# The head of an encoder step: no dummy products on TensorE ahead of the first turns, and a wait in front of GpSimd's first low halves

## The chip, the cores and the metric

The kernel runs on one core of a Trainium2 chip. The metric is the time of one execution in microseconds (us) on the device. Runs without the profiler give a median; one more execution was taken with the profiler, and all rows below come from that one. Engines: TensorE (PE, with PEld its weight loads), VectorE (DVE), ScalarE (ACT), GpSimd (POOL), SyncE (SP). TensorE's clock is granted at one of two levels, 2.4 GHz (1.00 in the rows) and 1.2 GHz (0.50).

## The reference

One inference step of an encoder layer over 256 prompt frames and 64 sample frames (320 tokens of width 1024), everything in float32:

```
x  = layer_norm(x, ln_in_g, ln_in_b)                  # the head: what this study is about
z  = x @ w_in                                         # q, k, v, u, vs, ga, gb
A  = chunk_attention(q, k, v, relative bias, cache)   # 8 heads x 64
B  = gelu(u) * (tril(W_s) @ layer_norm(gelu(vs)) + b_s)
m  = sigmoid(ga) * (A @ w_branch_a) + sigmoid(gb) * (B @ w_branch_b)
x  = layer_norm(ALPHA * x + m @ w_out)
x  = layer_norm(ALPHA * x + MoE(x))                   # 64 experts, top 8, and a shared one
x  = x + sigmoid(x @ ple_w_gate) * (p @ ple_w_proj)
```

## The kernel before

The program is written by hand, engine by engine, with semaphores; each engine executes its own list in order, and what an engine waits for is in the `wait_ge` in front of an instruction. The 320 tokens lie as three row blocks `t` of 128, 128 and 64 rows (`xs`).

Products that have to be exact to float32 are made of two parts: a high half (a copy of the value in a shorter format, made by ScalarE) and a low half (value minus high half). A weight tile of 1024 x 128 is split in two halves of four 128 x 128 blocks. ScalarE's `high` makes the high half of one (semaphore `w_high`), VectorE's `low` (L938) or GpSimd's `low_half` (L539) the low half (`w_low`). Each 128 x 128 block then takes three products on TensorE (`products`, L1347): high by high, high by low and low by high. The low halves of the first tile of `w_in` are GpSimd's, those of the next ones VectorE's.

The head, in the order of the work:

- SP loads the three row blocks, the two vectors of the first normalization, two chunks of `w_in` and the key cache. Each later chunk is loaded when `w_low` says that its place is free.
- VectorE makes the statistics of the three blocks (`norm_statistics`, which raises `var_ready`), then centres (`centre`, L902) and scales (`scale`, L912) each block. Both are operations on two SBUF operands. Each scaled block raises `ln_done`.
- ScalarE takes the square root of the variances, then makes four high halves (tiles 0 and 1, L634).
- TensorE waits for the constants and for `var_ready`, executes `WARM` = 16 products of the identity with itself into a bank that is not used yet (`keep_warm`, L1321), and then, for each block, waits for `ln_done` and turns the block with eight transposes (`transpose_rows`, L1313). ("Turn" stands for such a transpose below.) Eight turns of the key cache follow (L1333).
- For each turned block ScalarE copies the high part out of PSUM (`high_tile`, L644), and VectorE subtracts it from the PSUM block to make the low part (`low_xT`, L945: one PSUM operand and one SBUF operand); this raises `xT_ready`.
- TensorE waits for all three `xT_ready`, and enters the loop of the input projection (`project`), in its first part 20 tiles of 24 products.
- GpSimd makes constants, then the two low halves of tile 0 as soon as their high halves are there, then pads the relative-bias rows (L547), stores them (L549) and starts six strided loads of them (L556), each at a given count of `w_low`.

Behind the head follow attention, gating, the branch and output products, the routing, 16 expert steps, and the last normalization with its gate.

Of the kernel before, what the change touches and what calls it, by code (L numbers as in the profile page):

```python
# [34 lines left out]
P = 128  # L35
# [11 lines left out]
def trunk_step(nc, x_prompt, x_sample, cache_k, cache_v, p_prompt, p_sample, ln_in_g, ln_in_b, w_in,  # L47
# [30 lines left out]
    with ExitStack() as ctx:  # L78
        def sb(name, shape, dt=F32):
            return ctx.enter_context(nc.sbuf_tensor(name, shape, dt))  # L80

        def sem(name):
            return ctx.enter_context(nc.semaphore(name))
# [19 lines left out]
        ident = sb("ident", [P, P])  # L103
# [18 lines left out]
        PS = ctx.enter_context(nc.psum_tensor("PS", [P, 8, 512], F32))  # L122
# [133 lines left out]
        var_ready = sem("var_ready")  # L256
        std_ready = sem("std_ready")
        ln_done = sem("ln_done")
# [100 lines left out]
        PLE_BANK = (6, 7)  # L359
        MEAN_BANK, VAR_BANK = 5, 6  # L360

        WARM = 16
        GATE_GROUPS = ((0, 4), (4, 6), (6, 8))
        GATE_ORDER = [(0, 0), (0, 1), (1, 0), (1, 1), (2, 0), (3, 0), (2, 1), (3, 1)] + [(t, h) for t in range(4, KD) for h in range(2)]
        SCAT_BANK = (2, 3, 7, 0, 1, 3, 7, 0)
# [156 lines left out]
        def _(pool):  # L522
# [13 lines left out]
            def low_half(raw, part, signal):  # L536

                part = part.rearrange("p h (k n) -> p h k n", k=4)
                pool.tensor_tensor(part[:, 1, :, :], raw, part[:, 0, :, :].bitcast(F32), ALU.subtract).then_inc(signal, 1)  # L539


            for half in range(2):
                pool.wait_ge(w_high, half + 1)
                low_half(wr[:, 0, 4 * half:4 * half + 4, 0:P], split[:, half, :, :], w_low)
# [764 lines left out]
        def _(pe):  # L1309
# [4 lines left out]
                                       src[0:ROWS[t], t, P * k:P * (k + 1)], ident[0:ROWS[t], 0:ROWS[t]])  # L1314
                ins.then_inc(signal, 1)

            def keep_warm(n, bank):


                for _ in range(n):  # L1320
                    pe.matmul(PS[:, bank, 0:P], ident[:, :], ident[:, :], start=True, stop=True)  # L1321

            pe.wait_ge(const_ready, 1)
            pe.wait_ge(var_ready, 1)
            keep_warm(WARM, 7)
            for t in range(3):
                pe.wait_ge(ln_done, t + 1)
                transpose_rows(xs, t, 2 * t, xT_ps)
# [78 lines left out]
            for w in range(2):  # L1407
                if w:
                    pe.wait_ge(score_ready, 4)
                for h in range(4 * w, 4 * w + 4):  # L1410
                    par, i = h % 2, h // 2
                    for c, (key, n) in enumerate(((ckT[64 * par:64 * par + 64, i, :], 256), (head(K0, h, slice(256, TOK)), DH))):
                        ins = pe.matmul(PS[0:DH, 4 + 2 * par + i % 2, 256 * c:256 * c + n], query(h, 2), key,
                                        start=True, stop=True)
# [6 lines left out]
            for t in range(3):  # L1421
                n = ROWS[t]
                for g in range(8):
                    par = slice(64 * (g % 2), 64 * (g % 2) + 64)
                    ins = pe.matmul(PS[par, g // 2, cols(t)], vn[0:n, t, 64 * g:64 * g + 64], wsT[0:n, g, 0:n],
                                    start=True, stop=True)
# [103 lines left out]
            for k in range(KD):  # L1530
                for wp, xp in ((0, 0), (0, 1), (1, 0)):
                    at = (wp * KD + k) * NE
                    ins = pe.matmul(PS[:, 6, 0:TOK], marks[:, at:at + P], xT[:, xp, k, :], start=(k == 0 and (wp, xp) == (0, 0)),  # L1533
                                    stop=(k == KD - 1 and wp == 1))
# [250 lines left out]
```

## Time and profile before

| | |
|---|---|
| median of 3 runs | 880.78 us (880.29 to 881.53) |
| the profiled execution | 884.98 us |
| its span, first to last instruction | 882.9 us |
| busy: TensorE, its weight loads | 828.3 us (94%), 570.9 us (65%) |
| busy: VectorE, ScalarE, GpSimd | 383.6 us (43%), 269.1 us (30%), 36.4 us (4%) |
| the chain that ended last | TensorE 87%, VectorE 6%, DMA 2%, ScalarE 2% |
| mean granted clock of TensorE | 0.976 |

The profiled execution is 4.2 us longer than the median of the others, and 2.1 us of it lie outside of the span. The chain of waits follows the end of the kernel back: at each step to what released an instruction, or to the instruction before it on its engine. The shares of an engine's busy time are means over stages that are quite unlike each other; in the head, the first 23 us, TensorE waits for others for much of the time.

### The profile page before, as it was taken

What the parts mean: (1) busy time and instruction counts of PE and PEld (TensorE: products, weight loads), DVE (VectorE), ACT (ScalarE), POOL (GpSimd) and SP (SyncE); (2) the same over time, 40 slices, a digit from 0 to 9 for tenths busy, and PEclk for the clock granted to TensorE, in tenths of its full rate; (3) what the DMA queues carried; (4) which work ended last, traced back from release to release, by engine and by line L of the source; (5) the groups of instructions that cost most, each with busy time, mean ns of one, the idle gap of its engine ahead of it and who ended that gap; (6) DMA issues with size and microseconds to landing.
All of it is one profiled execution on the core that took longest, in us unless ns stands there. A gap on an engine that the chain in (4) does not pass through costs nothing.

```text
span 882.9 us, 13490 instructions
## 1 busy us (share of the span) xinstructions
PE 828.3 (94%) x4959; PEld 570.9 (65%) x4959; DVE 383.6 (43%) x846; ACT 269.1 (30%) x501; POOL 36.4 (4%) x50
## 2 busy tenths in 40 slices
PE   4999899889888999999999999999999999979877
PEld 4999799879877754654644655555464464542577
DVE  7434575737567714314404423422431441340574
ACT  2334466733443631211220221121121022020443
POOL 3001100000001220000000000000000000000000
PEclk9899999979999999999999999999999999998989
DMA  7496424437753079999999999999999999995001
GB/s 227 135 268 203 158 94 148 161 110 271 293 166 144 1 289 385 424 390 381 425 384 383 424 384 386 403 405 386 381 425 387 382 425 385 384 421 201 2 1 61
DMA packets 66042, 249.02 MB, mean 282 GB/s; under 512 B 5856, under 2 KB 37040, under 8 KB 41440
## 3 DMA queue, kind: packets, MB, share of 16 engines
q1 hardware_dynamic: 64848, 244.70, 70.6%
q0 software_dynamic: 1152, 3.95, 1.5%
q8 instruction: 17, 0.28, 0.1%
q10 hardware_dynamic: 16, 0.02, 0.0%
q14 instruction: 9, 0.07, 0.0%
HBM read 245.62 MB, written 3.03 MB: 282 GB/s over the span
## 4 chain that ended last, share of the span: by engine, by line
PE 87%; DVE 6%; DMA 2%; ACT 2%; issue 2%; SPq 1%; ACTq 0%; DVEq 0%; PEldq 0%
PE PS L1600 26%; PE PS L1347 21%; PE PS L1616 13%; PE PS L1630 9%; PE PS L1571 9%; PE PS L1721 3%; DMA weight_ring<-in_shared_w_dram 1%; DVE xs L912 1%; PE PS L1609 1%; DVE xs L902 1%; DMA expert_ring<-in_ln_in_b_dram 1%; PE PS L1579 1%; SPq L474 1%; PE PS L1533 1%; DVE parts L1183 1%
## 5 line engine op out<-in xcount | busy, mean ns | idle before, releaser
L1600 PE MATMUL PS<-expert_ring,z 128*64 128x512 f32 x1024 | 226.6, 600 | 6.3 <-issue 6.3
L1347 PE MATMUL PS<-parts,split 128*128 128x320 f32 x1344 | 203.0, 313 | 6.3 <-DVE parts L1067 3.3
L1347 PEld LDWEIGHTS PS<-parts,split 128*128 128x128 f32 x1344 | 201.1, 191 | 7.4 <-PEq L1490 3.5
L1600 PEld LDWEIGHTS PS<-expert_ring,z 128*64 128x64 f32 x1024 | 72.6, 138 | 147.7 <-issue 147.4
L1616 PE MATMUL PS<-expert_ring,z 128*64 128x512 f32 x512 | 115.4, 603 | 0.8 <-ACT z L787 0.8
L938 DVE TENSOR_TENSOR split<-weight_ring,split 128x512 fp32r<-128x512 f32 x106 | 73.8, 705 | 90.3 <-ACT split L634 90.0
L1223 DVE TENSOR_TENSOR split<-PS,split 128x512 fp32r<-128x512 f32 x64 | 44.3, 692 | 144.0 <-ACT split L792 143.6
L634 ACT ACTIVATE split<-weight_ring 128x512 fp32r<-128x512 f32 x112 | 69.9, 631 | 114.8 <-PE PS L1347 98.5
L783 ACT ACTIVATE z<-PS 128x256 f32<-128x256 f32 x32 | 12.3, 384 | 285.4 <-PE PS L1600 285.4
L1210 DVE SCALAR_TENSOR_TENSOR z<-PS,z 128x256 f32<-128x256 f32 x32 | 15.5, 484 | 191.5 <-ACT z L783 191.5
L1571 PEld LDWEIGHTS PS<-marks,parts 128*128 128x128 f32 x640 | 78.7, 191 | 14.0 <-issue 13.8
L1571 PE MATMUL PS<-marks,parts 128*128 128x256 f32 x640 | 85.0, 287 | 0.0
L1630 PEld LDWEIGHTS PS<-marks,split 128*128 128x128 f32 x512 | 75.2, 188 | 14.1 <-issue 13.0
L1630 PE MATMUL PS<-marks,split 128*128 128x320 f32 x512 | 80.5, 314 | 0.0
L1616 PEld LDWEIGHTS PS<-expert_ring,z 128*64 128x64 f32 x512 | 35.1, 138 | 67.4 <-issue 67.2
L792 ACT ACTIVATE split<-PS 128x512 fp32r<-128x512 f32 x64 | 38.3, 598 | 83.0 <-PE PS L1616 83.0
L1227 DVE TENSOR_TENSOR z<-z,PS 128x320 f32<-128x320 f32 x128 | 54.3, 484 | 11.7 <-PE PS L1630 10.1
L768 ACT ACTIVATE z<-PS 128x512 f32<-128x512 f32 x64 | 38.2, 597 | 47.8 <-PE PS L1571 47.8
L1721 PE MATMUL PS<-parts,split 128*128 128x320 f32 x192 | 31.7, 328 | 5.9 <-DVE parts L1273 4.8
L1721 PEld LDWEIGHTS PS<-parts,split 128*128 128x128 f32 x192 | 30.7, 204 | 6.7 <-issue 5.3
L1164 DVE TENSOR_TENSOR marks<-z 128x256 fp32r<-128x256 f32 x51 | 18.6, 420 | 6.5 <-PE PS L1571 6.0
L1164 DVE TENSOR_TENSOR z<-z 128x256 bf16<-128x256 f32 (+1 forms) x51 | 18.4, 416 | 0.0
(227 smaller groups left out, 527.6 us busy)
## 6 DMA issues: line engine op xcount, KB each, us to landing
expert_ring<-in_exp_w_dram SPq DMA_DIRECT2D x192, 1024.0 KB, 10.0
weight_ring<-in_w_in_dram SPq DMA_DIRECT2D x36, 512.0 KB, 4.4
weight_ring<-in_w_out_dram SPq DMA_DIRECT2D x8, 512.0 KB, 4.5
expert_ring<-in_ple_w_gate_dram SPq DMA_DIRECT2D x2, 2048.0 KB, 10.3
weight_ring<-in_w_branch_a_dram SPq DMA_DIRECT2D x4, 512.0 KB, 3.6
weight_ring<-in_w_branch_b_dram SPq DMA_DIRECT2D x4, 512.0 KB, 4.6
weight_ring<-in_shared_w_dram SPq DMA_DIRECT2D x4, 512.0 KB, 7.5
xs<-in_x_prompt_dram SPq DMA_DIRECT2D x2, 512.0 KB, 4.5
```

What stands on the lines that cost most here:

```text
L634: nc.scalar.activation(split[:, 2 * (place % 2) + half, 0, :].rearrange("p (k n) -> p k n", k=4), raw, ACT.Copy)\
L768: nc.scalar.activation(xgT[:, 2 * g:2 * g + 2, :].rearrange("p k s -> p (k s)"), PS[:, g % 2, :], ACT.Copy)\
L792: nc.scalar.activation(ysplit[:, j, 0, 512 * half:512 * half + 512], PS[:, 5 + half, :], ACT.Copy)\
L938: nc.vector.tensor_tensor(parts[:, 1, :, :], raw, parts[:, 0, :, :].bitcast(F32), ALU.subtract).then_inc(w_low, 1)
L1223: nc.vector.tensor_tensor(ysplit[:, j, 1, c], PS[:, 5 + half, :], ysplit[:, j, 0, c].bitcast(F32), ALU.subtract).then_inc(y_low, 1)
L1227: nc.vector.tensor_tensor(accT[:, q, :], accT[:, q, :], PS[:, SCAT_BANK[q], 0:TOK], ALU.add)\
L1347: ins = pe.matmul(out, w[:, wp, :], xT[:, xp, k0 + k, :], start=(start and k == 0 and (wp, xp) == (0, 0)), stop=(stop and k == 3 and wp == 1))
L1571: ins = pe.matmul(PS[:, g % 2, 256 * k:256 * k + 256], xrows[:, part, t, 2 * g + k, :], pick[:, t, :], start=(t == 0 and part == 0), stop= ...
L1600: ins = pe.matmul(PS[c, 2 + j, :], xgT[:, k, P * j + 64 * e:P * j + 64 * e + 64], w13(j, e, k), start=(k == 0), stop=(k == KD - 1))
L1616: ins = pe.matmul(PS[c, 5 + half, :], hidT[:, j, k, c], w2(j, e, k, half), start=(k == 0), stop=(k == 1))
L1630: ins = pe.matmul(PS[:, SCAT_BANK[q], 0:TOK], ysplit[:, j, part, P * q:P * (q + 1)], scat[:, j, 0:TOK], start=(j == 0 and part == 0), stop ...
L1721: ins = pe.matmul(PS[:, tile % 2, 0:TOK], w[:, wp, :], xT[:, xp, k, :], start=(k == 0 and (wp, xp) == (0, 0)), stop=(k == KD - 1 and wp == 1))
```

## The change

Two things are changed. TensorE no longer waits for `var_ready` and executes no dummy products; its first instruction on data is the first turn, when the first scaled block is there. And GpSimd waits for all three scaled blocks (`ln_done` 3) before the low halves of tile 0, which it made before as soon as their high halves were there. Everything that GpSimd does behind these is in the same order as before.

```diff
-        WARM = 16
...
+            pool.wait_ge(ln_done, 3)
             for half in range(2):
                 pool.wait_ge(w_high, half + 1)
                 low_half(wr[:, 0, 4 * half:4 * half + 4, 0:P], split[:, half, :, :], w_low)
...
-            def keep_warm(n, bank):
-
-
-                for _ in range(n):
-                    pe.matmul(PS[:, bank, 0:P], ident[:, :], ident[:, :], start=True, stop=True)
-
             pe.wait_ge(const_ready, 1)
-            pe.wait_ge(var_ready, 1)
-            keep_warm(WARM, 7)
             for t in range(3):
                 pe.wait_ge(ln_done, t + 1)
                 transpose_rows(xs, t, 2 * t, xT_ps)
```

## Rows read from the trace of the kernel before

**Rows 1.** Chain of waits, first 60 us: start us, us, what.

```profile
15.64 4.45 DVE xs L912 x2
...
22.28 0.68 DVE parts L945
...
23.44 36.63 PE PS L1347 x231
```

**Rows 2.** Timeline, VectorE: start us, us, engine, line, operation, out<-in, count.

```profile
13.18 1.28 DVE L912 SCALAR_TENSOR_TENSOR xs<-xs,rstd,expert_ring 128x1024 f32<-128x1024 f32 x1
...
15.57 2.30 DVE L912 SCALAR_TENSOR_TENSOR xs<-xs,rstd,expert_ring 128x1024 f32<-128x1024 f32 x1
...
17.80 2.29 DVE L912 SCALAR_TENSOR_TENSOR xs<-xs,rstd,expert_ring 64x1024 f32<-64x1024 f32 x1
...
20.02 2.94 DVE L945 TENSOR_TENSOR parts<-PS,parts 128x1024 fp32r<-128x1024 f32 x3
```

**Rows 3.** Timeline, GpSimd (in brackets: idle before, and what ended it).

```profile
14.44 2.36 POOL L539 TENSOR_TENSOR split<-weight_ring,split 128x512 fp32r<-128x512 f32 x1 [12.34 <-ACT split L634]
...
16.75 2.26 POOL L539 TENSOR_TENSOR split<-weight_ring,split 128x512 fp32r<-128x512 f32 x1
...
35.22 0.84 POOL L556 DMA_DIRECT2D expert_ring<-rel_rows  x1 [14.04 <-DVE split L938]
```

**Rows 4.** Line 539, the whole kernel: ns least, median and most.

```profile
L539 POOL TENSOR_TENSOR split<-weight_ring,split x6: 1297/1350/2356, 14.4 to 288.0; 128x512 fp32r<-128x512 f32 x6
```

**Rows 5.** Timeline, TensorE, from the dummies to the cache turns.

```profile
10.16 6.26 PE L1321 MATMUL PS<-ident 128*128 128x128 f32 x32 [10.16 <-DVE vareps L898]
16.26 1.04 PE L1313 MATMUL PS<-ident,xs 128*128 128x128 f32 x8
...
20.79 1.09 PE L1333 MATMUL PS<-ident,expert_ring 128*128 128x128 f32 x8
```

**Rows 6.** Timeline, ScalarE.

```profile
13.72 2.19 ACT L634 ACTIVATE split<-weight_ring 128x512 fp32r<-128x512 f32 x4 [3.47 <-DMA weight_ring<-in_w_in_dram]
17.33 1.02 ACT L644 ACTIVATE parts<-PS 128x1024 fp32r<-128x1024 f32 x1 [1.42 <-PE PS L1313]
...
20.89 0.60 ACT L644 ACTIVATE parts<-PS 128x512 fp32r<-128x512 f32 x1 [0.81 <-PE PS L1313]
```

**Rows 7.** Timeline at 255.7: GpSimd and VectorE at the same time.

```profile
255.74 1.28 POOL L596 TENSOR_TENSOR marks<-z,marks 128x512 fp32r<-128x512 f32 x1 [30.69 <-ACT marks L727]
256.18 1.22 DVE L1089 SCALAR_TENSOR_TENSOR xs<-xs,PS 128x1024 f32<-128x1024 f32 x1 [0.70 <-PE PS L1500]
```

**Rows 8.** Timeline at 177, TensorE: turns at the half clock.

```profile
176.80 0.64 PE L1435 MATMUL PS<-ident,expert_ring 128*128 128x128 f32 x2
...
177.23 0.42 PE L1433 MATMUL PS<-ident,expert_ring 128*128 128x128 f32 x1
```

**Rows 9.** Busy time by stretch: us, each engine (x), PEclk, DMA share, GB/s.

```profile
10.16:15.31 5.15, 5.15 (x24) 5.15 (x25) 4.60 (x5) 1.68 (x5) 0.87 (x1) 1.00 1.10 355
15.31:22.13 6.82, 4.81 (x42) 4.03 (x41) 6.82 (x5) 3.25 (x5) 5.57 (x4) 1.00 0.23 79
...
23.44:28.96 5.52, 5.52 (x21) 5.52 (x22) 2.60 (x5) 0.63 (x1) 0.00 (x0) 0.50 0.59 193
28.96:40.00 11.04, 11.04 (x77) 11.04 (x77) 4.15 (x6) 4.77 (x9) 0.84 (x1) 1.00 0.38 129
...
175.73:182.29 6.56, 4.68 (x36) 3.91 (x36) 3.29 (x6) 3.06 (x4) 0.00 (x0) 0.50 0.01 2
182.29:185.97 3.68, 3.68 (x28) 3.18 (x28) 1.10 (x3) 1.25 (x2) 0.00 (x0) 0.50 0.00 0
...
223.52:226.93 3.41, 3.24 (x12) 3.27 (x13) 2.84 (x8) 0.45 (x2) 1.53 (x7) 0.50 0.98 342
...
274.32:278.13 3.81, 3.81 (x16) 3.81 (x17) 2.94 (x6) 0.43 (x1) 0.00 (x0) 0.55 0.91 357
```

**Rows 10.** The same view, 17 to 18 us.

```profile
17.00:18.00 1.00, 0.37 (x4) 0.13 (x3) 1.00 (x2) 0.67 (x1) 1.00 (x1) 1.00 0.04 14
```

## The prediction

> **What bounds the kernel now.** I read the page first: TensorE is busy for most of the span, so a change at the head pays only by the time at which TensorE's long row of products begins, and by the clock that these products then get. Next the chain of waits over the first 60 us [rows 1]: it runs through VectorE's scaled rows (L912) and the low halves of xT (L945), and passes to TensorE at 23.44, where the projection products (L1347) begin and hold the chain without a break for 36.63 us. The quantity to predict is thus this one start, now 23.44, plus the cost of the clock behind it.
>
> Then VectorE's timeline [rows 2]: the first scaled row block takes 1.28 us, the next two 2.30 and 2.29. GpSimd's timeline [rows 3] shows why: its two low halves run from 14.44 to 16.80 and from 16.75 to 19.01, 2.36 and 2.26 us, where the median of that line is 1.35 and its least 1.30 [rows 4]. The ends interlock: VectorE's 15.57 + 2.30 = 17.87 is GpSimd's first end 16.75 plus 1.1; GpSimd's 19.01 is 17.87 plus 1.1; VectorE's 17.80 + 2.29 = 20.09 is 19.01 plus 1.1. The two engines take turns, each waiting for the whole of the other's instruction. TensorE's timeline [rows 5]: 32 dummy pieces from 10.16 end where the first turns begin, at 16.26, although the first scaled rows were ready at 13.18 + 1.28 = 14.46. Last, ScalarE [rows 6]: its four high halves keep it until 15.91, then each block's high part takes 1.02 us (0.60 for the 64 rows).
>
> **The change part by part.**
>
> *GpSimd's wait for ln_done 3.* VectorE's second scaled block starts at 15.57 as before and takes 1.28, to 16.85; the third starts 0.07 before that end (as 17.80 stands to 17.87), and takes 1.28, to 18.06. Before: 20.09. VectorE gains 2.03 us.
> What stands behind the waiting instruction on GpSimd: both low halves (tile 0's), the 64-column copy and the DMA of the relative-bias rows, then the strided bias loads. Low halves at 18.1 to 19.45 and to 20.8; TensorE wants them when its products begin, VectorE's own low halves of tile 1 wait for them (w_low 2) behind the last L945. Both come after 21.8 (below), so 1 us of cover is left; without it every us late would be a us lost. The bias loads waited 14.04 us for VectorE's w_low count [rows 3], so 2 us later there is hidden. No DMA of SP's stands behind GpSimd's wait but the next weight chunk (w_low 4), which follows VectorE's tile 1 and moves with it.
> Do the low halves now collide with L945 instead? L945 reads PSUM and one SBUF operand. The nearest row: GpSimd's two-operand subtraction at 255.74 took 1.28 us while VectorE's L1089, also one PSUM and one SBUF operand, ran over it in 1.22 [rows 7]. Nothing lost; I take 0. The other end is in the rivals.
>
> *No dummies.* Their 16 products of two pieces each go. They kept TensorE 1.8 us past the ready rows, which was covered, since the chain went through VectorE. What they gave: pieces ran at 5.15 / 24 = 0.215 us until 15.31 and the granted clock was full from there to 22.13 [rows 9], 2.4 GHz, so the turns ran at 1.04 us for eight [rows 5]. Without them I take the turns at half clock, 1.2 GHz. Rows for a turn at half: two take 176.80 to 177.23, 0.215 each [rows 8]. So eight cost 8 x 0.215 = 1.72 plus about 0.3 of first start and tail = 2.0, instead of 1.04.
> - t = 0: 14.5 to 16.5; ScalarE free since 15.91, high part to 17.55; VectorE's L945 waits for its own 18.06 anyway.
> - t = 1: rows at 16.85, turns 16.9 to 18.9; ScalarE 18.95 to 19.97; L945 from 20.0. Three L945 took 2.94, the last 0.68 [rows 1, 2], so the first two 1.13 each: to 21.13.
> - t = 2: rows at 18.06, turns behind those of t = 1, begun at 18.65, at most 2.0 long: 20.6; ScalarE to 21.2 at the latest; L945 0.68, to 21.85.
> - the cache turns (L1333), behind them on TensorE: about 8 x 0.215 = 1.72 from 20.4 at the latest, so issued by 22.1; they do not wait for their DMA: from 17 to 18 the DMA share is 0.04 [rows 10].
> The products began 0.48 after the last L945 (22.28 + 0.68 = 22.96 to 23.44 [rows 1]); now 21.8 + 0.48 = 22.29. Gain **1.15 us**. Bounds of this term: had the turns full clock, the chain would be VectorE alone, 18.02 + 2.94 = 20.96, products at 21.45, gain 2.0; with the cache turns last at half clock, 22.1 + 0.48, gain 0.85.
>
> *The clock behind the start.* In the profiled execution the products ran at half clock from 23.44 to 28.96, 5.52 us [rows 9]: 21 in 5.52 us, 0.263 each, against 77 in 11.04, 0.143. Each us at half clock costs 1 - 0.143 / 0.263 = 0.455 us; the stretch cost 2.5. With the dummies 7 us away, that clock had already fallen at 22.13, after turns with pauses between them, so the dummies bought nothing for the products here. How long is the new stretch? From the start of steady work to the rise, rows give 5.15 (dummies), 5.52, 3.68 (182.29 on), 3.41 and 3.81 [rows 9]. The three short ones are nearer in one respect: in two of them TensorE had worked shortly before, as it now does from 14.5 to 22 with pauses of some 0.4 us. I take 4.0, between the three (mean 3.6) and all five (4.3). Gain (5.52 - 4.0) x 0.455 = **0.7 us**; bounds 0 (5.52 again) and 1.0 (3.41).
>
> This is where a rule of the Trainium skill speaks against me. The rows first: at 175.73 to 182.29 the clock stayed at half through turns, a pause and attention products; then turns and products ran without a pause from 182.29 and it was full at 185.97 [rows 9]. More than half of that stretch is turns, so turns seem to help the clock up. The Trainium skill, page "TensorE: Matmul & The Clock Gate", Part 4: PE-mode transpose, says the opposite: the full clock does not engage for transposes. By that rule the new turns would leave the clock cold and the clock's term would be 0, a sum of 1.15 us; by the row it is 1.85. The row is mixed work, so it does not settle it.
>
> **Sum.** 1.15 + 0.7 = 1.85 us earlier. Behind 23.44 TensorE is the chain and everything up to the last store counts from its products, so the shift is carried to the end. The profiled execution took 884.98 (span 882.9 and 2.1 around it): 883.1. The runs' median, 880.78, is 4.2 lower; the head is a difference of starts, so I carry it over unchanged: **878.9 us**. A measurement of this kernel tells about 0.2%, 1.76 us, from no change: the forecast stands almost on that line.
>
> **The rivals.**
> - *Clock as before.* The start moves, the half-clock stretch stays 5.5 us (the turns don't count, or the median run had a shorter stretch than the profiled one anyway, so there is less to win). Gain 0.85 to 1.3: 879.6. For it: both rows that start from a long quiet (5.15, 5.52). Against: the three short ones.
> - *The turns bring the clock up and the products keep it.* Steady turns from 14.5 to 22 raise it by about 18 to 21, and it holds over the 0.7 us pause. Then 1.15 to 2.0 plus most of 2.5: gain 3.0 to 4.0, 877.3. For it: the 182.29 row. Against: the clock fell at 22.13 and again by 175.73 after turns with pauses.
> - *GpSimd blocks L945 instead.* If L945 takes turns with the low halves as L912 did, 18.06 + 1.13 (L945), + 1.3, + 1.13, + 1.3, + 0.68 gives 23.6, products at 24.1: 0.65 slower, less the clock's 0 to 0.7: 881.0. Against it: rows 7.
> - *Slower.* Without dummies the full clock comes back much later. The longest half-clock stretch in the trace is 175.73 to 185.97, 10.24 us; that long behind 22.29 would cost (10.24 - 5.52) x 0.455 = 2.15, less 1.15: 1.0 slower, 881.8. It decides from 5.52 + 1.15 / 0.455 = 8.0 us on. For more than 0.2% it would have to be 12 us, which no row shows.
> - *Nothing comes through.* A later wait takes up the 1 to 2 us: 880.8. Against it: 36.63 us of unbroken products behind the start.
>
> **How the numbers follow.** Forecast (1.5 to 2.3 earlier, 878.5 to 879.3) 0.42; clock as before 0.26; clock kept 0.17; L945 blocked 0.05; late clock 0.06; nothing 0.04. Faster by over 0.2% (below 879.0): some 0.28 of the forecast's, all of the kept clock's, 0.03 of the second: 0.48. Slower by over 0.2%: 0.05, the tails of the late clock, the blocked L945 and what I have not seen. Same: 0.47. The range takes in the first three cases with the bounds of their terms and some of the spread of the runs shown (1.2 us): 876.9 to 880.6; 15% are left out, above it for the most part.
>
> **What would show it.** Right: L912 three times at 1.28, the last over by 18.1; low halves of 1.3 to 1.4 at 18.1 and 19.4; L945 of unchanged length, the last over by 21.9; first L1347 at 22.3; half clock behind it for some 4 us. Wrong: turns of t = 1 that end after 19.2 (half-clock price too low), L945 over 2 us (blocked), products later than 22.7 (cache turns or low halves last), or a half-clock stretch of 5.5 us or more.

## The result, and the profile after

The changed kernel takes 874.29 us (median of 13 executions, 868.63 to 878.46), the kernel before 882.9 us (13 executions, 880.29 to 887.22): ratio 0.9893, 95% interval 0.9871 to 0.9914. (The 880.78 us from which the forecast started was the median of three of these 13.) By the ratio that is some 9.4 us where 1.85 were forecast, and the time lies outside of the range. The profiled execution of the changed kernel took 874.54 us, with a span of 872.5.

The head first. The chain of waits of the changed kernel, first 60 us, for [rows 1]:

```profile
16.38 1.98 PE PS L1314 x8
...
20.59 0.69 DVE parts L946
...
21.76 23.10 PE PS L1340 x144
```

Its timelines of VectorE, GpSimd and TensorE, for [rows 2, 3, 5]:

```profile
10.21 1.28 DVE L903 SCALAR_TENSOR_TENSOR xs<-xs,meanvar,expert_ring 128x1024 f32<-128x1024 f32 x1 [0.44 <-DMA expert_ring<-in_ln_in_b_dram]
...
15.06 2.46 DVE L913 SCALAR_TENSOR_TENSOR xs<-xs,rstd,expert_ring 128x1024 f32<-128x1024 f32 x2
17.45 1.21 DVE L946 TENSOR_TENSOR parts<-PS,parts 128x1024 fp32r<-128x1024 f32 x1
19.45 1.82 DVE L946 TENSOR_TENSOR parts<-PS,parts 128x1024 fp32r<-128x1024 f32 x2 [0.79 <-ACT parts L645]
```

```profile
17.61 2.51 POOL L538 TENSOR_TENSOR split<-weight_ring,split 128x512 fp32r<-128x512 f32 x2 [15.51 <-DVE xs L913]
```

```profile
14.09 1.94 PE L1314 MATMUL PS<-ident,xs 128*128 128x128 f32 x8 [14.09 <-DVE xs L913]
16.38 3.01 PE L1314 MATMUL PS<-ident,xs 128*128 128x128 f32 x16 [0.35 <-DVE xs L913]
19.33 1.97 PE L1326 MATMUL PS<-ident,expert_ring 128*128 128x128 f32 x8
```

The second and third scaled blocks now take 2.46 us together, the two low halves 2.51, and L946 (L945 before) is as long as it was. Eight turns take 1.94 us in place of 1.04: half clock. The products begin at 21.76, 1.68 us earlier. The first centring began 0.50 us earlier in this execution (10.21 against 10.71, released by the load of ln_in_b), so the change's own part is 1.18 us.

The clock behind the start, busy time by stretch, for [rows 9] (the last three numbers of a row are PEclk, DMA share and GB/s; no clock is recorded before 25.55, so the 1.00 of the first row says nothing, and the pace tells the clock):

```profile
21.76:25.55 3.79, 3.79 (x14) 3.79 (x15) 1.91 (x4) 0.19 (x1) 0.00 (x0) 1.00 0.54 171
25.55:36.59 11.04, 11.04 (x77) 11.04 (x76) 4.16 (x6) 5.09 (x10) 0.84 (x1) 1.00 0.44 141
```

14 products in 3.79 us are 0.27 each, half clock; then 77 in 11.04 as before. The stretch is 3.79 us, where it was 5.52.

At the prediction's 0.455 for each us these 1.73 us are worth 0.79, so the head is some 2.0 us ahead, close to the 1.85 forecast, and no more. The rest lies 760 us later. The chain of waits from 780 to 830, the kernel before:

```profile
788.34 0.50 DVE z L1227
788.84 5.75 issue
794.59 16.83 PE PS L1600 x64
...
811.45 0.39 ACT z L783
...
813.92 8.80 PE PS L1616 x32
822.72 4.95 PE PS L1630 x32
```

and the changed kernel:

```profile
787.92 0.50 DVE z L1228
788.42 0.19 issue
788.61 13.97 PE PS L1593 x64
...
802.61 0.39 ACT z L784
...
805.07 7.10 PE PS L1609 x32
812.17 4.96 PE PS L1623 x32
```

"issue" is time in which the engine waited for nothing that the profile shows. At 788.34 the two executions are 0.42 us apart; at the next product they are 5.98 apart (794.59 against 788.61), at 811.45 and 802.61 8.84, at 822.72 and 812.17 10.55. All of these 10.1 us fall into the last expert step: 5.6 into a gap in front of its first product, 2.9 into its first 64 products, and 1.7 into 32 later ones (8.80 us against 7.10). Why those are slower is in the busy time by stretch, kernel before:

```profile
788.32:794.59 6.27, 0.00 (x0) 0.00 (x1) 2.23 (x6) 0.00 (x0) 0.00 (x0) 0.92 1.00 413
794.59:811.42 16.83, 16.80 (x64) 5.13 (x64) 0.48 (x1) 0.38 (x1) 0.00 (x0) 0.83 0.38 135
...
814.03:817.44 3.41, 3.41 (x10) 1.01 (x12) 0.00 (x0) 0.00 (x0) 0.00 (x0) 0.50 0.81 327
```

TensorE does nothing for 6.27 us, the clock falls inside of the gap, and the 64 products behind it take 16.83 us where they take 13.97 in the changed kernel. The 32 later ones meet a second half-clock stretch, 814.03 to 817.44, which the changed kernel's profile does not have; that the gap caused this one too is not shown (see e1 and e3).

What TensorE has to do at this place: the expert steps are a loop; behind it stands code for extra rounds, for experts with over 64 tokens, over which TensorE jumps with these inputs (`pe.If(more > 0)`); the jump's target is the last step. In the kernel before, the DMA queue that carries instructions moved nothing between 788.4 and 791.9, and one packet between 791.9 and 793.2 (DMA queues in the two stretches: packets, MB, share of 16 engines):

```profile
q1 hardware_dynamic: 195, 1.47, 100.5%
...
q1 hardware_dynamic: 80, 0.53, 100.9%
q8 instruction: 1, 0.02, 4.9%
```

The first product follows 1.4 us behind that stretch. The changed kernel, too, moves a packet there, and no earlier: none between its loop's last product (787.89) and 791.3, and one between 791.3 and 792.6,

```profile
q8 instruction: 1, 0.02, 4.9%
```

but its TensorE has work in the meantime. Over the whole kernel this queue, q8, has 17 packets before and 16 after (page, DMA queues); that it is TensorE's is inferred from this, since the other queue for instructions, q14, has 9 in both:

```profile
q8 instruction: 17, 0.28, 0.1%
```

```profile
q8 instruction: 16, 0.26, 0.1%
```

The 32 dummy pieces are 32 MATMUL and 32 LDWEIGHTS, 64 instructions that stand ahead of all else in TensorE's program. So the theory: without them everything behind moves forward in the program by 64 places, the jump's target falls into code that is already loaded, and the gap goes, with the half clock that it caused. The rival: the gain comes from the head, and the gap went because the last step was reached in another state.

### The profile page after: what moved, and what is told of

The parts are those of the page before. It is cut to its first block, busy times and chain, and to the rows that moved or that the text cites. A ratio compares the mean times of both kernels' runs of the same rounds, so it can differ in the third digit from the quotient of the medians.

```text
span 872.5 us, 13427 instructions
## 1 busy us (share of the span) xinstructions
PE 819.9 (94%) x4927; PEld 565.9 (65%) x4927; DVE 381.5 (44%) x846; ACT 269.1 (31%) x501; POOL 33.3 (4%) x50
## 4 chain that ended last, share of the span: by engine, by line
PE 86%; DVE 6%; DMA 3%; ACT 2%; SPq 1%; issue 1%; ACTq 0%; PEldq 0%; DVEq 0%
PE PS L1593 26%; PE PS L1340 20%; PE PS L1609 13%; PE PS L1623 9%; PE PS L1564 9%; PE PS L1714 4%; DMA weight_ring<-in_w_in_dram 1%; DMA weight_ring<-in_shared_w_dram 1%; PE PS L1602 1%; DVE xs L903 1%; PE PS L1572 1%; DMA expert_ring<-in_ln_in_b_dram 1%; PE PS L1526 1%; DVE xs L913 1%; DVE parts L1184 1%
## 5 line engine op out<-in xcount | busy, mean ns | idle before, releaser
L1593 PE MATMUL PS<-expert_ring,z 128*64 128x512 f32 x1024 | 223.7, 594 | 0.7 <-DVE z L1228 0.7
L1609 PE MATMUL PS<-expert_ring,z 128*64 128x512 f32 x512 | 113.7, 596 | 0.8 <-ACT z L788 0.8
L1228 DVE TENSOR_TENSOR z<-z,PS 128x320 f32<-128x320 f32 x128 | 54.3, 484 | 11.7 <-PE PS L1623 10.1
L1314 PE MATMUL PS<-ident,xs 128*128 128x128 f32 (+1 forms) x48 | 7.8, 326 | 15.7 <-DVE xs L913 15.7
```

The lines of the kernel that those rows point to most:

```text
L1228: nc.vector.tensor_tensor(accT[:, q, :], accT[:, q, :], PS[:, SCAT_BANK[q], 0:TOK], ALU.add)\
L1593: ins = pe.matmul(PS[c, 2 + j, :], xgT[:, k, P * j + 64 * e:P * j + 64 * e + 64], w13(j, e, k), start=(k == 0), stop=(k == KD - 1))
L1609: ins = pe.matmul(PS[c, 5 + half, :], hidT[:, j, k, c], w2(j, e, k, half), start=(k == 0), stop=(k == 1))
```

## The experiments

All ratios are to the kernel before, run on the same chip in turn. The expectations count the gap on the engine's weight loads (6.55 us before, 0.99 changed), the table as "issue" in the chain of waits. By the pages the changed kernel executes 13,427 instructions, e3 13,491, f4 13,459 and f2 13,682; the +9 of a loop is taken from the expectations, and no trace shows it.

| kernel | TensorE's instructions against the changed kernel | gap in front of the last step's first product, "issue" | ratio, 95% interval |
|---|---|---|---|
| before | +64 | 5.75 | 1 |
| changed | 0 | 0.19 | 0.9893 (0.9871 to 0.9914) |
| changed, again (g1) | 0 | 0.19 | 0.9891 (0.9865 to 0.9917) |
| wait alone (e1) | +64 | 5.75 | 0.9978 (0.9953 to 1.0002) |
| no dummies alone (e2) | 0 | 0.15 | 0.9891 (0.9853 to 0.9930) |
| code without work (e3) | +64 | 6.03 | 0.9965 (0.9940 to 0.9989) |
| work, little code (e4) | +9 | 0.19 | 0.9900 (0.9872 to 0.9927) |
| no jump (f1) | no jump | 0.34 | 0.9888 (0.9864 to 0.9912) |
| 255 more (f2) | +255 | 0.21 | 0.9881 (0.9855 to 0.9907) |
| dummies in a loop and wait (f3) | +9 | 0.17 | 0.9886 (0.9859 to 0.9912) |
| 32 more (f4) | +32 | 0.20, and 1.60 further on | one execution: 875.5 us |
| ten dummies in a loop and wait (g2) | +9 | 0.16 | 0.9899 (0.9867 to 0.9931) |
| dummies in a loop and wait, again (g3) | +9 | 0.17 | 0.9885 (0.9859 to 0.9911) |

**The wait alone (e1_wait_alone).** The kernel before with one line more:

```diff
+            pool.wait_ge(ln_done, 3)
             for half in range(2):
                 pool.wait_ge(w_high, half + 1)
```

> The kernel before with GpSimd's wait alone; the 16 dummies stay. Theory (most of the gain is a stall that lies at the jump out of the expert loop, and that went because TensorE's program is 64 instructions shorter): the gap of some 6 us in front of the last expert step's first product stays, with half clock behind it; only the head gains, 1 to 2 us: ratio 0.997 to 1.000. Rival (the gain comes from the head: earlier products, a shorter half-clock stretch there): L912 at 1.28 three times brings most of the gain, ratio 0.992 or less.

Measured: 879.8 us, ratio 0.9978. The chain of waits at the last step:

```profile
784.67 0.50 DVE z L1228
785.17 5.75 issue
790.92 15.72 PE PS L1601 x64
```

The gap is there to the hundredth, and the 64 products behind it take 15.72 us where they take 13.97 in the changed kernel. The head has more than the changed kernel's gain (L912 at 1.28, 1.27 and 1.27, products 10.68 us behind the first centring where it was 12.73 before, and at full clock from the first) and brings 0.2%, with an interval that just includes nothing. The rival, 0.992 or less, falls.

**No dummies alone (e2_no_dummies_alone).** The kernel before without the dummies:

```diff
             pe.wait_ge(const_ready, 1)
-            pe.wait_ge(var_ready, 1)
-            keep_warm(WARM, 7)
```

> The kernel before without the dummies; GpSimd's low halves as early as before. Theory of the jump: TensorE's program is as short as the changed one's, so the gap in front of the last expert step is under 1 us and no half-clock stretch follows it; the head gains nothing or loses up to 0.5 us by slow turns: ratio 0.989 to 0.993. Rival (the head): VectorE and GpSimd still take turns, products begin at 23.4 or later, ratio 0.998 to 1.002.

Measured: 875.22 us, ratio 0.9891, the whole gain. L912 takes 2.30 and 2.29 as before, and the products begin 12.72 us behind the first centring as before. The chain at the last step:

```profile
790.49 0.50 DVE z L1227
790.99 0.15 issue
791.14 9.22 PE PS L1598 x41
```

**Code without work (e3_code_no_work).** The changed kernel with 64 instructions that wait for nothing (the compiler makes 64 of the 129 waits):

```diff
+            for _ in range(129):
+                pe.wait_ge(const_ready, 1)
             pe.wait_ge(const_ready, 1)
             for t in range(3):
```

> The changed kernel with 64 more instructions for TensorE at its start that do nothing: waits on a count that is long reached, done by about 6 us, while TensorE has nothing to do until 14. TensorE's program is again as long as that of the kernel before, without any product. Theory of the jump: the gap of some 6 us in front of the last expert step is back, 8 to 10 us are lost against the changed kernel: ratio 0.997 to 1.000. Rival (the work of the dummies or the head matter): as the changed kernel, ratio 0.989.

Measured: 879.91 us, ratio 0.9965. No dummy product is executed, the waits are over before the first scaled rows, the products begin 11.54 us behind the first centring as in the changed kernel, and the gap is back:

```profile
787.77 0.50 DVE z L1228
788.27 6.03 issue
794.30 15.65 PE PS L1595 x64
```

The loss against the changed kernel is some 6.3 us by the two ratios, less than the 8 to 10 that were expected: the clock behind the gap cost 1.7 us in this profile (15.65 against 13.97) and 1.8 in e1's, where the profile of the kernel before lost 4.6 to its two half-clock stretches. With the gap in place and the changed kernel's own head, 0.35% is left (interval 0.11 to 0.60%).

**Work with little code (e4_work_little_code).** The kernel before with its dummies in a loop:

```diff
-            keep_warm(WARM, 7)
+            with pe.Fori(0, WARM):
+                keep_warm(1, 7)
```

> The kernel before with its 16 dummies in a loop: the same work at the same place, in a program some 55 instructions shorter. GpSimd's low halves early. Theory of the jump: the gap in front of the last expert step is under 1 us as in the changed kernel, ratio 0.989 to 0.993, unless the 9 instructions by which it is longer than the changed kernel's already move the jump's target out. Rival (the dummies' work costs the time): as before, ratio 0.998 to 1.002.

Measured: 874.32 us, ratio 0.9900, "issue" 0.19 us in front of the last step. All 32 pieces are executed in the same place. With e3 this is the crossing: the code without the work costs, the work without the code does not.

**No jump (f1_no_jump).** The kernel before without TensorE's code for extra rounds; it leaves out the work for experts with over 64 tokens, of which these inputs have none:

```diff
-            with pe.If(more > 0):
-                with pe.Fori(0, more) as r:
-                    with pe.Fori(0, STEPS) as i:
-                        expert_step(r * STEPS + i + STEPS - 1, 4 * i)
             expert_step(more * STEPS + STEPS - 1, None, last=True)
```

> The kernel before, dummies and all, but TensorE's code for the extra expert rounds is left out, over which it jumps with these inputs (so it could not serve an expert with more than 64 tokens). No jump, the last expert step follows the loop directly. Theory (the stall is the jump's: its target is not yet loaded): the gap of 6.6 us in front of the last step falls under 1.1, no half clock behind it, ratio 0.988 to 0.993, though the head is that of before. Rival (the stall is a wait for data or for another engine at the last step, which the changed kernel meets by luck of its earlier start): the gap stays.

Measured: 872.6 us, ratio 0.9888. The last step follows the loop at once, with dummies and head as before (L912 2.30 and 2.29, products 12.73 us behind the first centring):

```profile
785.20 0.34 issue
785.54 13.97 PE PS L1600 x64
```

So no wait for data or another engine makes the gap; it comes with the jump over that code. (The jump and the code were taken out together; the changed kernel also jumps, and has 0.19.)

**255 more (f2_255_more).** The changed kernel with:

```diff
             pe.wait_ge(const_ready, 1)
+            for _ in range(128):
+                pe.matmul(PS[0:1, 7, 0:1], onesb[:, 0:1], onesb[:, 0:1], start=True, stop=True)
```

> The changed kernel with 255 more instructions for TensorE at its start: 128 tiny products (1 by 1 column), done before the first scaled rows. The instruction queue's packets carry 16,384 bytes each, which would be 256 instructions of 64 bytes. Theory of place (what counts is where the jump and its target lie within such blocks): nearly one whole block more leaves the places as in the changed kernel, gap of about 1 us, ratio 0.988 to 0.992. Rival (a longer program stalls, whatever the place): gap over 6 us, ratio 0.996 to 1.000.

Measured: 873.01 us, ratio 0.9881, "issue" 0.21 us: a program longer than that of the kernel before, and no gap. Length alone doesn't make it; the place does. The trace gives 16,384 bytes for each packet, and this kernel's q8 has 17 of them where the changed kernel has 16. How many instructions one holds, no trace shows. The Trainium skill, page "Advanced Engine Details and Errata", section "ISA Cache", gives 16 KB and 256 instructions for such a line; this run agrees with it at one point, a shift by nearly one such line.

**32 more (f4_32_more).** As e3, with half as many:

```diff
+            for _ in range(65):
+                pe.wait_ge(const_ready, 1)
```

> The changed kernel with 32 more instructions for TensorE that do nothing (waits on a count that is long reached, done by 6 us). With 0 and with 9 more the gap was 1.04 us, with 64 more 6.6 to 6.9. Theory of place: one of the two values, none between: the target either has been loaded or has not. Rival (the fetch is a matter of time, and each instruction more delays it): some 3 to 4 us.

Measured in one execution: 875.5 us. Neither value, and not the rival's either. The chain:

```profile
785.56 0.20 issue
785.76 3.64 PE PS L1595 x15
789.40 1.60 issue
791.01 9.23 PE PS L1595 x41
```

The jump costs nothing, the first 15 products run, and then TensorE waits 1.60 us. The expectation of one of two values was wrong. The reading that fits all of these runs is finer: the target now lies 15 products in front of the end of what is loaded; the next packet is moved only behind the jump (between 788.4 and 789.6, some 3.4 us behind the loop's last product, as in the changed kernel; 3.6 before); and what is executed in the meantime covers a part of the wait. An estimate from these rows: the wait to be covered is 3.64 + 1.60 = 5.24 us, and a product is two instructions (MATMUL and LDWEIGHTS). So 32 fewer, the changed kernel, leave 31 products, 6.8 us at 13.97 / 64 each, which is enough; 32 more, e3, leave none.

**Dummies in a loop and the wait (f3_loop_and_wait, and again as g3).** Both edits of e1 and e4:

> Dummies in a loop (9 instructions more than in the changed kernel) and GpSimd's wait: the turns at full clock and a short program. Head as in the run with the wait alone: products some 0.9 us earlier than in the changed kernel, counted from VectorE's first centring (10.7 us against 11.55), half clock behind them 0 to 4 us; gap at the last step about 1 us. Ratio 0.986 to 0.991, 0.5 to 2 us under the changed kernel if the start at 2 us of difference in the head is carried to the end, equal to it if the later half-clock stretches take it up.

Measured: 872.24 us, ratio 0.9886. Products 11.09 us behind the first centring, 0.46 earlier than in the changed kernel (0.9 were expected), and no half clock behind them. To see whether this is worth anything, three kernels were run beside each other on one chip: the changed kernel, ten dummies in a loop with the wait, and this one.

> The changed kernel as it is, beside the next two on one chip. Ratio 0.987 to 0.992; half clock behind the first products for 1 to 4 us.

> Ten dummies in a loop instead of sixteen, and GpSimd's wait: 20 pieces of 0.215 from var_ready end when the first scaled rows are ready, instead of some 2 us later. If the dummies' clock is what helps the head, no half clock behind the first products as in the run with sixteen in a loop, and the first product 0.4 us earlier than there: 10.7 us behind VectorE's first centring. If ten are too few to bring the clock up, turns and products at half as in the changed kernel. Ratio 0.985 to 0.991 or as the changed kernel.

> Sixteen dummies in a loop and GpSimd's wait, again, beside the changed kernel. In the profile its 60th product lay 20.0 us behind the first centring against 22.2 in the changed kernel. If this is carried to the end, 1 to 2 us under the changed kernel; if the later half-clock stretches take it up, equal within the interval.

Measured: 872.48, 872.41 and 872.27 us; ratios 0.9891 (0.9865 to 0.9917), 0.9899 (0.9867 to 0.9931) and 0.9885 (0.9859 to 0.9911). No difference. In the three profiles the products had come to the same point, 60 on, 20.1, 21.2 and 21.2 us behind the first centring, the changed kernel earliest; in the profiles shown above it had been 22.2 for the changed kernel and 20.0 for this one. The changed kernel had no half clock behind its first products here, where 1 to 4 us were expected. The head's clock differs from one execution to the next by more than these edits move it. As ten in a loop were to do, the first product came 10.71 us behind the first centring, but half clock was back behind it for 3.4 us; neither of the two cases expected.

## Why the prediction was wrong

*The head: right in place; what it is worth in time is not settled.* VectorE's last scaled block was forecast to be over at 18.06 and was at 17.52, which is 18.02 with the 0.50 us of the earlier first centring; the last L945 at 21.85, measured 20.59 + 0.68 and 0.50, 21.8; the products at 22.29, measured 21.76 and 0.50, 22.26. Turns of 0.215 us each, no blocking of L945 by GpSimd (1.21 and 1.23 us), all as worked out. The kernel with this head and the old length of the program is e3: 0.9965, which is 3.1 us (1.0 to 5.3) where the sum was 1.85. The wait alone, e1, gives 0.9978, 1.9 us (nothing to 4.1), by a head that starts earlier still. Both agree with the sum, and neither proves its size.

*The clock behind the start: right on this execution, in part by luck.* 4.0 us forecast, 3.79 measured. But it is one draw of several: the changed kernel run again had no half clock there at all. Its busy time by stretch:

```profile
14.70:18.25 3.55, 3.14 (x14) 2.77 (x15) 3.55 (x4) 2.41 (x4) 0.00 (x0) 1.00 0.64 220
18.25:22.11 3.86, 2.12 (x20) 1.65 (x19) 3.39 (x4) 1.51 (x2) 3.36 (x4) 1.00 0.00 0
22.11:26.00 3.89, 3.89 (x26) 3.89 (x27) 2.60 (x5) 0.70 (x2) 0.00 (x0) 1.00 0.56 174
```

Its record of the clock begins at 18.25 with full clock, 3.5 us into the turns, with nothing but turns executed until then; and the products have it from their first (26 in 3.89 us). In e3, too, turns alone came to full clock, and the cache turns take 1.09 us; there it had fallen again when the products began (12 in 3.29 us):

```profile
17.64 2.61 PE L1314 MATMUL PS<-ident,xs 128*128 128x128 f32 x16 [0.35 <-DVE xs L913]
20.18 1.09 PE L1328 MATMUL PS<-ident,expert_ring 128*128 128x128 f32 x8
```

The rule of the Trainium skill that the prediction weighed (page "TensorE: Matmul & The Clock Gate", Part 4: PE-mode transpose: full clock does not engage for transposes) agrees with the first profile of the changed kernel, where 7 us of turns did not bring it, and is contradicted by these two, where turns alone did. As a price it was not needed: whichever way it went, no more than 2.5 us hung on it.

*The step that failed: what the removed dummies cost.* The prediction priced them as time on TensorE ("covered, since the chain went through VectorE") and as clock ("bought nothing for the products here"), and said that behind 23.44 "everything up to the last store counts from its products". It left out that they are 64 instructions, and that their place in the program moves all the rest. Of the gain of 1.07%, some 0.35% (e3, with its interval) are left for the two terms of the sum, and the rest is a term that the sum did not have: e2 has the whole gain without the head's, e3 loses most of it again with no work added, e4 has it with all of the work. What the runs showed in its place: with these 64 instructions ahead, TensorE stands idle for 5.75 to 6.03 us at the jump to the last expert step and then loses 1.7 to 2.9 us to the half clock; without them it waits 0.15 to 0.19. The rivals named only what could follow the head in time, none what could follow it in the program.

*Could it have been seen?* The gap could. The page of the kernel before has the line

```profile
L1600 PE MATMUL PS<-expert_ring,z 128*64 128x512 f32 x1024 | 226.6, 600 | 6.3 <-issue 6.3
```

6.3 us of idle time in front of the costliest group, released by "issue", that is, by nothing in the profile; for a line that is executed 1024 times this is one single wait (the view of waits from 780 to 822 has it, once, with 6.3 us). Asking where it stands leads to the jump. That a shift by 64 instructions would end it could not be read from one trace; it would have been a rival with a price (6 us of gap and the half clock behind it) and a chance that nothing pinned down.

*Carried to the end: open.* The head's lead of some 2.4 us between the two profiled executions (98 products by 40.00 before, 91 by 36.59 after) was down to 0.42 at 788: half-clock stretches at 175.7, 223.5 and 274.7 stand in both records at the same time from the start of the span, and the kernel that is earlier meets them with other work. Over many runs e3 still shows 0.35%, so this may be spread and not loss. But the kernels without the gap are alike whether they have the head's gain (0.9881 to 0.9899) or not (e2, e4 and f1: 0.9888 to 0.9900), within intervals of 0.2 to 0.4% to either side. How much of the forecast 1.85 us arrives at the end was not shown.

## What to carry to other kernels

Instructions that are added or removed have two prices: what they do, and that everything behind them moves in the program. Where an engine jumps over code, look for idle time that ends by "issue", and test a change's gain with its code but not its work (waits that are long satisfied) and its work but not its code (a loop), before it is put down to the work. A profiled half-clock stretch at the head is one draw: five profiled executions with the changed kernel's order of work there (the changed kernel twice, e3, f2 and f4) had it for 3.8, 0, 3.3, 3.5 and 1.2 us.

## What the runs showed of the hardware that was not expected

- A jump to code that, as the runs are read here, was not loaded cost TensorE 5.75 to 6.03 us, three times (before, e1, e3), and 2.9, 1.8 and 1.7 us more by the clock that fell in the gap. In the kernel before, the packet of instructions that ended it was moved only 3.6 us after TensorE had nothing left to do, though the queue had moved nothing since 376 us; in the changed kernel and in f4, too, the next packet was moved only behind the jump, some 3.4 us after the loop's last product.
- The price is not all or nothing: with the target 15 products in front of the end of the loaded code it was 1.60 us.
- GpSimd and VectorE take turns whole instruction by whole instruction where both read two SBUF operands (2.30 and 2.36 us for 1.28 and 1.30), and not at all where VectorE reads one and PSUM (1.21 and 1.23 beside low halves of 1.28 and 1.27 in the changed kernel).
